# A mixer's eigenvalue computation on GpSimd, moved from the first layer's attention steps to its gate and up projections

## The reference

```
proj = x @ w_in                              # q, k, v of both attentions, gates
ya = neighbourhood_attention(...)            # 8 heads
yb = bidirectional_retention(...)            # 4 heads, decay tables
y = (sigmoid(gate_a) * (ya @ w_a) + sigmoid(gate_b) * (yb @ w_b)) @ w_out
x = layer_norm(alpha * x + y)
ffn = (gelu(conv(x @ w_up)[a]) * conv(x @ w_up)[b]) @ w_down
x = layer_norm(alpha * x + ffn + sigmoid(x @ w_gate) * (p @ w_proj))
```

```
dt = exp(log_dt)
mag = exp(lam_re * dt)
abar_r, abar_i = mag * cos(lam_im * dt), mag * sin(lam_im * dt)
coef = (abar - 1) / lam                      # complex
```

## Time and profile before

| | |
|---|---|
| median of 3 runs | 2397.57 us (2396.03 to 2398.3) |
| the profiled execution | 2396.23 us, span 2394.4 us |
| PE busy | 2319.3 us, 97% of the span |
| DVE, ACT busy | 978.4 and 975.8 us, 41% each |
| POOL busy | 1123.5 us, 47%; of it 378 low parts, 921.7 us |
| chain that ended last | PE 88%, DVE 6%, ACT 2%, POOL 2% |

### The profile page before, as it was taken

The page is one execution under the profiler, slowest core; times in us unless marked ns, Lnnn a source line. Parts: engine busy times, 40 slices in busy tenths (PEclk is TensorE's granted clock), DMA queues, the critical chain, the costliest instruction groups (busy, mean ns, idle before and its releaser), DMA issues.

```text
span 2394.4 us, 32622 instructions
## 1 busy us (share of the span) xinstructions
PE 2319.3 (97%) x11792; PEld 1906.4 (80%) x11792; DVE 978.4 (41%) x1527; ACT 975.8 (41%) x1328; POOL 1123.5 (47%) x684
## 2 busy tenths in 40 slices
PE   7999999999999998999999999999999989999998
PEld 6878888878888886888888877888887767888886
DVE  6364353342443203543552243434375685222201
ACT  4444343243555414444443234555512425434321
POOL 5787434544444453333334445343454665444452
PEclk9999999999999999999999999999999999999999
DMA  5212222322322432222223223233333112232331
GB/s 189 77 61 68 94 79 95 99 72 96 100 93 97 132 97 64 85 82 80 62 85 97 89 78 97 96 93 100 97 107 105 46 36 87 97 103 91 104 97 53
DMA packets 61137, 214.16 MB, mean 89 GB/s; under 512 B 7184, under 2 KB 7440, under 8 KB 61072
## 3 DMA queue, kind: packets, MB, share of 16 engines
q1 hardware_dynamic: 58480, 205.39, 26.6%
q10 hardware_dynamic: 2592, 7.87, 1.0%
HBM read 211.13 MB, written 2.10 MB: 89 GB/s over the span
## 4 chain that ended last, share of the span: by engine, by line
PE 88%; DVE 6%; ACT 2%; POOL 2%; issue 2%; SPq 0%; DMA 0%; ACTq 0%; DVEq 0%; POOLq 0%
PE psum L750 84%; PE psum L866 1%; DVE z L1778 1%; DVE states L1972 1%; PE psum L853 1%; POOL w_lo L419 1%; ACT z L1350 0%; ACT xh L1349 0%; DVE s_t L1602 0%; PE psum L832 0%; DMA convp<-in_convp 0%; PE psum L965 0%; PE psum L1066 0%; PE psum L918 0%; DVE xm_lo L1786 0%
## 5 line engine op out<-in xcount | busy, mean ns | idle before, releaser
L419 POOL TENSOR_TENSOR w_lo<-stage,w_hi 128x1024 fp32r<-128x1024 f32 x378 | 921.7, 2448 | 1204.1 <-ACT w_hi L1194 1190.2
L750 PE MATMUL psum<-xh,w_hi 128*128 128x512 f32 x1888 | 742.1, 393 | 16.0 <-DVE xl L2122 8.2
L750 PE MATMUL psum<-xl,w_hi 128*128 128x512 f32 x1888 | 737.4, 391 | 0.0
L750 PE MATMUL psum<-xh,w_lo 128*128 128x512 f32 x1888 | 736.8, 390 | 0.0
L1194 ACT ACTIVATE w_hi<-stage 128x1024 fp32r<-128x1024 f32 x377 | 396.3, 1052 | 353.2 <-PE psum L750 351.5
L750 PEld LDWEIGHTS psum<-xh,w_hi 128*128 128x128 f32 x1888 | 355.6, 188 | 99.5 <-issue 17.1
L750 PEld LDWEIGHTS psum<-xh,w_lo 128*128 128x128 f32 x1888 | 355.7, 188 | 74.9
L750 PEld LDWEIGHTS psum<-xl,w_hi 128*128 128x128 f32 x1888 | 355.9, 188 | 71.8
L750 PE MATMUL psum<-g_hi,w_hi 128*128 128x512 f32 x528 | 205.4, 389 | 0.0
L750 PE MATMUL psum<-g_lo,w_hi 128*128 128x512 f32 x528 | 205.4, 389 | 0.0
L750 PE MATMUL psum<-g_hi,w_lo 128*128 128x512 f32 x528 | 205.4, 389 | 0.0
(11 more groups left out here) (366 smaller groups left out, 3178.0 us busy)
## 6 DMA issues: line engine op xcount, KB each, us to landing
stage<-in_w SPq DMA_DIRECT2D x379, 512.0 KB, 3.4
bias<-in_bias ACTq DMA_DIRECT2D x8, 384.0 KB, 3.0
out_x<-out_t SPq DMA_DIRECT2D x4, 512.0 KB, 2.7
z<-in_x SPq DMA_DIRECT2D x3, 512.0 KB, 7.1
p_raw<-in_p ACTq DMA_DIRECT2D x2, 512.0 KB, 3.4
masks<-in_masks SPq DMA_DIRECT2D x1, 576.0 KB, 10.0
masks<-in_masks ACTq DMA_DIRECT2D x1, 576.0 KB, 5.0
stage<-in_w ACTq DMA_DIRECT2D x1, 512.0 KB, 4.8
```

The source lines that it names most:

```text
L419: pool.tensor_tensor(w_lo[s][:, :, :], stage[s][:, :, :], w_hi[s][:, :, :].bitcast(F32), ALU.subtract).then_inc(lo_done, 1)
L750: mm = pe.matmul(dst, lhs[i], rhs[j], start=start and n == 0, stop=stop and n == 2)
```

## The change

The eigenvalue blocks leave the first 32 units. They stand between the low parts of units 76 to 111 of layer 0, that is from the fifth unit of `ple` to the seventh iteration of `up` (units 106 to 109) and two units behind it. `growth_and_angle` is cut in two (`step_sizes` first). The temporary tiles move to the end of `g_lo`: its tiles 14 to 21, which the last 4 of the 11 `up` iterations write. This region also holds `ya_hi` and `p_raw` earlier in the layer. So `lam` is no longer loaded by SP at the start but by ACT, behind the rounding of unit 71 and a wait for `p`'s low part; `log_dt` keeps its load and gets its own semaphore. DVE's `up` loop is split into 7 and 4 iterations, and between them DVE waits for all powers. Everything else in the diff renames the tile `k` to `turns`.

```
-            sp.dma_start(lam[:, :, :], a["lam"]).then_inc(lam_in, 16)
-            sp.dma_start(dt[:, 0, :], a["log_dt"]).then_inc(lam_in, 16)
+            sp.dma_start(dt[:, 0, :], a["log_dt"]).then_inc(log_dt_in, 16)
...
+        eig_at = a_at + FT * T * 4 + EIG_TILE * T * 4          # EIG_TILE = 14
-        eig = [place(f"eig{i}", [P, LAM], offset=a_at + 16384 + LAM * 4 * i) for i in range(8)]
+        eig = [place(f"eig{i}", [P, LAM], offset=eig_at + LAM * 4 * i) for i in range(8)]
...
             pool.wait_ge(lo_done, 2)
-            low_parts(2, 4)
-            growth_and_angle()
-            low_parts(4, 6)
-            exp_rest(x, k, exp2[:, :])
-            low_parts(6, 9)
-            exp_series(mag, x, p, exp2[:, :])
-            low_parts(9, 13)
-            quarter_turns()
-            low_parts(13, 17)
-            series()
-            low_parts(17, 22)
-            turn()
-            low_parts(22, 26)
-            coefficients()
-            low_parts(26, 28)
-            phase_powers(range(N_POW // 2))
-            low_parts(28, 30)
-            phase_powers(range(N_POW // 2, N_POW))
-            low_parts(30, 32)
+            low_parts(2, 32)
...
-                with pool.Fori(base + OUT0 // RING + 3, base + down_round) as n:
+                first_round = OUT0 // RING + 3
+                if L == 0:
+                    u = first_round * RING
+                    low_parts(u, u + 3)
+                    step_sizes()
+                    low_parts(u + 3, u + 5)
+                    growth_and_angle()
+                    low_parts(u + 5, u + 6)
+                    exp_rest(x, turns, exp2[:, :])
+                    low_parts(u + 6, u + 9)
+                    exp_series(mag, x, p, exp2[:, :])
+                    low_parts(u + 9, u + 14)
+                    quarter_turns()
+                    low_parts(u + 14, u + 19)
+                    series()
+                    low_parts(u + 19, u + 25)
+                    turn()
+                    low_parts(u + 25, u + 30)
+                    coefficients()
+                    low_parts(u + 30, u + 32)
+                    phase_powers(range(N_POW // 2))
+                    low_parts(u + 32, u + 34)
+                    phase_powers(range(N_POW // 2, N_POW))
+                    low_parts(u + 34, u + 36)
+                    first_round += 9
+                with pool.Fori(base + first_round, base + down_round) as n:
...
+                if L == 0:
+                    act.wait_ge(p_lo_s, 1)
+                    act.dma_start(lam[:, :, :], a["lam"]).then_inc(lam_in, 16)
                 norm(L, 0)
...
-                with dve.Fori(0, FT // 2) as j:
+                if L == 0:
+                    with dve.Fori(0, EIG_TILE // 2) as j:
+                        up(L, j)
+                    dve.wait_ge(powers_ready, N_POW)
+                    dve.wait_ge(lam_step, lam_steps[0])
+                with dve.Fori(0 if L else EIG_TILE // 2, FT // 2) as j:
                     up(L, j)
```

More of the change, by code:

```diff
@@ L88 @@
 EXP_MAX, EXP_MIN = 88.0, -87.0
+EIG_TILE = 14
 EXP_C = [1 / 5040, 1 / 720, 1 / 120, 1 / 24, 1 / 6, 1 / 2, 1.0]
@@ L200, in build @@
         assert at[0] <= nc.sbuf_usable_end, (at[0], nc.sbuf_usable_end)
-        eig = [place(f"eig{i}", [P, LAM], offset=a_at + 16384 + LAM * 4 * i) for i in range(8)]
-        lam = place("lam", [P, 2, LAM], offset=a_at + 16384 + LAM * 32)
-        int_at = a_at + 16384 + LAM * 40
-        eig_tmp = place("eig_tmp", [P, LAM], offset=a_at + 16384 + LAM * 48)
+        eig_at = a_at + FT * T * 4 + EIG_TILE * T * 4
+        eig = [place(f"eig{i}", [P, LAM], offset=eig_at + LAM * 4 * i) for i in range(8)]
+        lam = place("lam", [P, 2, LAM], offset=eig_at + LAM * 32)
+        int_at = eig_at + LAM * 40
+        eig_tmp = place("eig_tmp", [P, LAM], offset=eig_at + LAM * 48)
+        assert LAM * 52 <= (FT - EIG_TILE) * T * 4
         exp2 = place("exp2", [P, LAM], mybir.dt.int32, offset=int_at)
@@ L307, in build @@
         c_in, b_in, wb_in, wp_in = sem("ssm_c_in"), sem("ssm_b_states_in"), sem("ssm_b_in"), sem("w_pool_in")
-        lam_in = sem("eigenvalues_in")
+        lam_in, log_dt_in = sem("eigenvalues_in"), sem("log_dt_in")
         mpar_in = sem("mixer_small_params_in")
@@ L332, in stand @@
             eng.sem_inc(passed, 1)
+        lam_steps = [0]
         def block_view(ap):
@@ L422, in _ @@
             tt, ts = pool.tensor_tensor, pool.tensor_scalar
-            lam_steps = [0]
             def step():
@@ L463, in exp_series, with step_sizes, growth_and_angle @@
                 pool.wait_ge(*settled())
-            x, mag, angle, k, p, y, sine, cosm1 = (e[:, :] for e in eig)
+            x, mag, angle, turns, p, y, sine, cosm1 = (e[:, :] for e in eig)
             chans, by_state = slice(0, SP_T * SN), slice(SP_T * SN, LAM)
             per_q = lambda v: v.rearrange("p (q n) -> p q n", n=SN)
-            def growth_and_angle():
-                pool.wait_ge(lam_in, 32)
+            def step_sizes():
+                pool.wait_ge(log_dt_in, 16)
                 exp_rest(dt[:, 0, :], dt[:, 1, :], exp2_dt[:, :])
                 exp_series(dt[:, 3, :], dt[:, 0, :], dt[:, 2, :], exp2_dt[:, :])
+            def growth_and_angle():
+                pool.wait_ge(lam_in, 16)
                 for part, dst in ((0, x), (1, angle)):
@@ L481, in quarter_turns @@
             def quarter_turns():
-                ts(k, angle, 1.0 / QUARTER, ROUND, ALU.mult, ALU.add).then_inc(*step())
+                ts(turns, angle, 1.0 / QUARTER, ROUND, ALU.mult, ALU.add).then_inc(*step())
                 pool.wait_ge(*settled())
-                ts(k, k, ROUND, None, ALU.subtract).then_inc(*step())
+                ts(turns, turns, ROUND, None, ALU.subtract).then_inc(*step())
                 for part in (QUARTER_HI, QUARTER_MID, QUARTER_LO):
                     pool.wait_ge(*settled())
-                    two_ops(out=angle, in0=k, scalar=-part, in1=angle, op0=ALU.mult, op1=ALU.add)
-                ts(p, k, 0.25, ROUND, ALU.mult, ALU.add).then_inc(*step())
+                    two_ops(out=angle, in0=turns, scalar=-part, in1=angle, op0=ALU.mult, op1=ALU.add)
+                ts(p, turns, 0.25, ROUND, ALU.mult, ALU.add).then_inc(*step())
                 pool.wait_ge(*settled())
@@ L493, in quarter_turns @@
                 pool.wait_ge(*settled())
-                two_ops(out=k, in0=p, scalar=-4.0, in1=k, op0=ALU.mult, op1=ALU.add)
+                two_ops(out=turns, in0=p, scalar=-4.0, in1=turns, op0=ALU.mult, op1=ALU.add)
                 pool.wait_ge(*settled())
@@ L512, in turn @@
                 pool.wait_ge(*settled())
-                tt(y, k, k, ALU.mult).then_inc(*step())
+                tt(y, turns, turns, ALU.mult).then_inc(*step())
                 pool.wait_ge(*settled())
@@ L518, in turn @@
                 tt(y, y, p, ALU.mult).then_inc(*step())
-                tt(k, k, eig_tmp[:, :], ALU.mult).then_inc(*step())
+                tt(turns, turns, eig_tmp[:, :], ALU.mult).then_inc(*step())
                 pool.wait_ge(*settled())
                 ts(y, y, -1.0, 1.0, ALU.mult, ALU.add).then_inc(*step())
-                ts(k, k, 1.0 / 3, None, ALU.mult).then_inc(*step())
+                ts(turns, turns, 1.0 / 3, None, ALU.mult).then_inc(*step())
                 pool.wait_ge(*settled())
@@ L527, in turn @@
                 pool.wait_ge(*settled())
-                two_ops(out=x, in0=x, scalar=1.0, in1=k, op0=ALU.add, op1=ALU.mult)
-                tt(angle, angle, k, ALU.mult).then_inc(*step())
+                two_ops(out=x, in0=x, scalar=1.0, in1=turns, op0=ALU.add, op1=ALU.mult)
+                tt(angle, angle, turns, ALU.mult).then_inc(*step())
                 two_ops(out=cosm1, in0=y, scalar=-1.0, in1=cosm1, op0=ALU.add, op1=ALU.add)
@@ L569, in phase_powers @@
                 t, nr, t2, u = (st[:, i, :] for i in range(6, 10))
-                pc, ps = k[:, by_state], p[:, by_state]
+                pc, ps = turns[:, by_state], p[:, by_state]
                 if levels[0] > 0:
```

## The result

The changed kernel takes 2406.81 us (median of 6 runs, 2405.37 to 2408.43) against 2397.93 us before: a ratio of 1.0039, 95% interval 1.0028 to 1.0049. It is slower, by 8.9 us. Its profiled execution took 2405.37 us with a span of 2403.3.

What follows compares the result with a forecast made beforehand. PE was taken to bound the kernel. From 2396.2 us: attention steps minus 13.7, startup minus 0.7, late low parts and slow clock plus 21.9, giving 2403.7; with 1.3 for the median, 2405.0 us, range 2389 to 2416.

Steps and rivals of the forecast that it cites:

- three attention steps: Layer 0's first three attention steps, freed of eigenvalue blocks, should match layer 1's: minus 13.7 us, bounds 9.4 to 13.7.
- opening, to the first scores: Startup without SP's early lam load: parameters arrive sooner, 0.7 us gained, bounds 0 and 2.5.
- wait ahead of unit 85: Gate and up projections: low part 85, behind an exponential series block, 0.6 us late for PE.
- 90: Gate and up projections: low part 90, behind the quarter turns, 0.7 us late for PE.
- 95: Gate and up projections: low part 95, behind the sine and cosine series, 3.7 us late, slow clock behind it.
- 101: Gate and up projections: low part 101, behind the turn block, 1.8 us late for PE.
- 108: Gate and up projections: low part 108, behind the first powers block, 1.4 us late for PE.
- 110: Gate and up projections: low part 110, behind the second powers block, 10.3 us late, slow clock behind it.
- slow clock behind the waits: Gate and up projections: matmuls at a lowered clock after two of PE's waits, 1.7 us each, 3.4 together.
- DVE's wait, the split loop, ACT's load: DVE's new wait for the powers, its loop's extra branch and ACT's lam load: cost 0, the load at most 0.4 us.
- Contention: Gate and up projections: POOL may hold DVE's two-input instructions up to 2.4 us; only in the upper bound, 1.2 us mean.
- Rival 1: The blocks fit in gate and up, PE never late, only the gain left: 2383 us; chance 0.12.

Runs made afterwards that it cites:

- e3: Kernel before with only SP's load of lam moved behind lnp and convp, eigenvalues still in the attention steps: 2396.66 us, ratio 0.9993.
- e1: Changed kernel without the eigenvalue blocks, their results filled with a constant, the rest of the change kept: 2382.10 us, ratio 0.9938 to before.
- e4: Changed kernel's eigenvalue instructions in the same order, in portions of about 2.7 us behind each low part, powers levels 1 to 7 behind units 110 to 116: 2384.25 us.
- e5: Kernel before, eigenvalues still in the attention steps but cut into portions of about 3.9 us behind the low parts of units 2 to 31: 2390.31 us.
- e8: As e4 but with thinner portions, 2.1 instead of 2.7 us behind each low part: 2382.58 us, ratio 0.9936 to before.
- e2: Changed kernel with the second half of the powers moved, one level behind each of units 112 to 115: 2399.34 us, ratio 1.0007 to before.

## Why the prediction was right, step by step

The forecast was 2405.0 us; 2406.8 was measured. Sign and mechanism held, and the experiments show late low parts to be the cause of the loss; the sizes are these.

| step | forecast | measured |
|---|---|---|
| three attention steps | -13.7 | -13.6 |
| opening, to the first scores | -0.7 | -2.1 |
| wait ahead of unit 85 | 0.6 | none |
| 90 | 0.7 | 1.7 |
| 95 | 3.7 | 3.1 |
| 101 | 1.8 | 2.5 |
| 108 | 1.4 | 3.3 |
| 110 | 10.3 | 7.4 |
| slow clock behind the waits | 3.4 | 4.8 |
| restarts, rest | not counted | 2.4 |

- *The waits.* 18.5 us in six against 18.0 in five. That the sums agree to 0.5 us is partly luck: the wait ahead of 110 was 2.9 us shorter than forecast, those ahead of 90, 101 and 108 together 3.6 longer. The term that was mis-sized most is the second powers block: I took its 16.4 us of the attention steps, where DVE disturbs it (there its instructions of 0.22 us take up to 0.75 beside DVE's rotation), and here it ran for 13.0 (713.7 to 726.7), like the first (13.6). The turn was 0.5 us longer than forecast, and the wait ahead of 101 0.7. The wait ahead of 108 was longer for two reasons: the first powers ran 0.5 us longer, and they began some 1.4 us nearer to PE's need, since POOL had to wait 2.3 us for high part 107, where the forecast had low part 107 right behind 106.
- *The clock.* The 1.7 us apiece was right (1.6), the count was not: it fell behind 95, 101 and 110, and I had counted 95 and 110 alone. What PE loses in starting again I left out.
- *The opening.* The 0.7 took the transfer alone, and that part came to 0.5 (PE starts the last unit ahead of the scores at 23.76 instead of 24.26 us). The other 1.6 are the slow clock behind PE's wait there, which the kernel before has (granted clock 0.72 from 24 to 30 us) and the changed one hasn't (1.00); the prediction named this case in its bound of 2.5. e3 shows that the order of loads brings these 2 us.
- *DVE's wait, the split loop, ACT's load: 0.* Right, by e1.
- *Contention.* DVE's products took 1055 ns on average, not 692, and cost PE nothing; nor did they at 1434 (e4). The Trainium skill ("SBUF — State Buffer", "Who interferes with whom") calls the port pair of DVE and GpSimd an exclusive lock, and has a DVE instruction with two SBUF inputs contend with a GpSimd instruction that reads SBUF. The rows agree: a mask with two such inputs ends 0.3 us behind POOL's low part (e5). That section of the Trainium skill words the hold for a whole instruction for DVE's two-port modes; the rows show it for this two-input instruction. e4 and e5 tell where it matters here: not in the gate and up projections, where DVE idles between two tiles, but in the attention steps, where PE's next bank hangs on the rotation behind the mask.
- *Rival 1* (the blocks fit) was wrong for these blocks and right for their sum: e8 puts the same instructions into the same stretch and its nearest units at no cost. The sum of POOL's work, 200 us in 203.5, looked hopeless, yet seven of the eight levels of the powers were free to move behind units 110 to 116, and the rest fits unit by unit.

## What to carry to other kernels

An engine that feeds a ring may take other work only in portions below the ring's lead at that very place, counted from the time at which its input arrives; the engine's idle share over the stage doesn't tell it. Here portions of about 3 us cost nothing, of 11 us 8 (at one place with a lead of 6.9 us; elsewhere 14.5 to 16.8 were free), of 22 us 45. Before moving work to an emptier stage, try cutting it up; and allow for a slow clock behind each wait of TensorE, which came here behind three of five.

## What the runs showed of the hardware that was not expected

- The granted clock fell to half behind a wait of PE of 2.5 us (unit 101, kernel after), and not behind one of 3.3 us (unit 108). Behind the longest, 7.4 us, no more matmuls were slow than behind that of 3.1. So by these rows a wait of 2.5 us or more cost 0 or 1.6 us beside itself and the restart.
- The same piece, from layer 0's first mean to the third gate unit, took 26.9 us in the profiles of before and after, 27.6 in e1's and 29.3 in e2's, with no edit there (granted clock 1.00, 1.00, 0.94 and 0.88). So two single profiles of this kernel can differ by 2.4 us in a piece that no edit touched.
- What holds DVE can be an instruction that was there all along: the masks shown, 2.55 us in the kernel before and 2.56 in e5 in place of 0.42, both end 0.3 us behind a low part of POOL, and not behind an instruction of the eigenvalue computation.
